# 512-column float32r matmuls of a transformer's projections as two of 256 columns on the same weights

## The reference

```python
h = rms_norm(x, norm1_gain[l]) * (1.0 + sc1) + sh1
z = h @ w_in[l]                       # 1024 x 4408
...
merged = sigmoid(g_mla_merge) * y_mla + sigmoid(g_nsa_merge) * y_nsa
x = x + gt1 * (merged @ w_out[l])
h2 = rms_norm(x, norm2_gain[l]) * (1.0 + sc2) + sh2
x = x + gt2 * ((silu(h2 @ ffn_w_gate[l]) * (h2 @ ffn_w_up[l])) @ ffn_w_down[l])
```

## Time and profile before

| | |
|---|---|
| median of 3 runs | 2311.57 us (2309.75 to 2312.49) |
| the profiled execution, first to last instruction | 2308.2 us |
| TensorE busy | 2253.8 us, 98% |
| weight loads busy | 1799.2 us, 78% |
| VectorE, ScalarE, GpSimd busy | 947.8, 612.0, 1393.4 us |
| matmuls recorded | 10597 |

### The profile page before, as it was taken

One profiled execution on the slowest core, in us unless ns is written; L12 is line 12 of the kernel. 1 busy time (PEld: TensorE's weight loads), 2 busy tenths in 40 slices (PEclk: granted clock), 3 DMA queues, 4 the chain that ended last, 5 costly groups with the idle time before them and its releaser, 6 DMA issues.

```text
span 2308.2 us, 28721 instructions
## 1 busy us (share of the span) xinstructions
PE 2253.8 (98%) x10597; PEld 1799.2 (78%) x10597; DVE 947.8 (41%) x1742; ACT 612.0 (27%) x1335; POOL 1393.4 (60%) x522
## 2 busy tenths in 40 slices
PE   7999999999999999999999999999999999999997
PEld 5787887787888888787787788888787787888885
DVE  6744777544110132325636433302235627433202
ACT  3263652112111100104643222201015623222200
POOL 4755404776777777774018777777773038777773
PEclk9999999999999999999999999999999999999999
DMA  8322103422222232222002222222221012222221
GB/s 327 128 74 92 56 20 114 176 80 75 103 91 91 96 146 109 92 91 73 1 19 73 105 95 91 92 91 91 91 91 55 1 37 74 94 101 96 91 91 55
DMA packets 32725, 206.08 MB, mean 89 GB/s; under 512 B 4080, under 2 KB 4336, under 8 KB 11632
## 3 DMA queue, kind: packets, MB, share of 16 engines
q1 hardware_dynamic: 32192, 200.27, 24.1%
q10 hardware_dynamic: 432, 4.46, 0.5%
HBM read 202.61 MB, written 2.10 MB: 89 GB/s over the span
## 4 chain that ended last, share of the span: by engine, by line
PE 92%; DVE 3%; POOL 1%; issue 1%; ACT 1%; DMA 0%; DVEq 0%; ACTq 0%; SPq 0%; POOLq 0%
PE PS L756 25%; PE PS L758 25%; PE PS L757 25%; PE PS L1052 5%; PE PS L1078 4%; PE PS L1067 2%; PE PS L1025 1%; PE PS L828 1%; PE PS L770 1%; POOL w_hi L426 1%; POOL w_lo L430 1%; PE PS L1108 1%; DVE ring L1997 1%; PE PS L1337 0%; DMA xT<-xT_dram 0%
## 5 line engine op out<-in xcount | busy, mean ns | idle before, releaser
L426 POOL TENSOR_TENSOR w_hi<-raw,zero_c 128x2048 fp32r<-128x2048 f32 (+1 forms) x238 | 593.7, 2508 | 834.0 <-PE PS L758 832.7
L430 POOL TENSOR_TENSOR w_lo<-raw,w_hi 128x2048 fp32r<-128x2048 f32 (+1 forms) x238 | 757.4, 3197 | 12.4
L756 PE MATMUL PS<-f_hi,w_hi 128*128 128x512 f32 x992 | 393.5, 397 | 2.1 <-POOL w_lo L430 1.4
L758 PE MATMUL PS<-f_hi,w_lo 128*128 128x512 f32 x992 | 393.3, 396 | 0.0
L757 PE MATMUL PS<-f_lo,w_hi 128*128 128x512 f32 x992 | 393.2, 396 | 0.0
L756 PEld LDWEIGHTS PS<-f_hi,w_hi 128*128 128x128 f32 x992 | 186.8, 188 | 48.8 <-POOL w_lo L430 2.3
L758 PEld LDWEIGHTS PS<-f_hi,w_lo 128*128 128x128 f32 x992 | 186.8, 188 | 45.6
L757 PEld LDWEIGHTS PS<-f_lo,w_hi 128*128 128x128 f32 x992 | 186.8, 188 | 45.3
L756 PE MATMUL PS<-a_hi,w_hi 128*128 (+1 forms) x528 | 209.7, 397 | 0.0
L757 PE MATMUL PS<-a_lo,w_hi 128*128 (+1 forms) x528 | 209.3, 396 | 0.0
L758 PE MATMUL PS<-a_hi,w_lo 128*128 (+1 forms) x528 | 209.3, 396 | 0.0
(11 more groups left out here) (424 smaller groups left out, 3692.4 us busy)
## 6 DMA issues: line engine op xcount, KB each, us to landing
raw<-slabs_dram SPq DMA_DIRECT2D x161, 1024.0 KB, 4.8
aux<-ada_dram SPq DMA_DIRECT2D x18, 512.0 KB, 5.1
ada_first<-ada_dram SPq DMA_DIRECT2D x11, 512.0 KB, 14.1
cmpw<-cmpw_dram ACTq DMA_DIRECT2D x2, 2048.0 KB, 11.6
ada_late<-ada_dram SPq DMA_DIRECT2D x8, 512.0 KB, 3.3
ada_last<-ada_dram SPq DMA_DIRECT2D x8, 512.0 KB, 6.1
xT<-xT_dram SPq DMA_DIRECT2D x1, 2048.0 KB, 9.1
out_dram<-t SPq DMA_DIRECT2D x4, 512.0 KB, 2.7
```

The source lines that it names most:

```text
L426: high = nc.gpsimd.tensor_tensor(w_hi[:, slot, c], raw[:, slot, c], zero[:, 0:c.stop - c.start], ALU.add)
L430: low = nc.gpsimd.tensor_tensor(w_lo[:, slot, c], raw[:, slot, c], w_hi[:, slot, c].bitcast(f32), ALU.subtract)
L756: nc.tensor.matmul(out, a_hi_, b_hi_, start=start, stop=False)
L758: return nc.tensor.matmul(out, a_lo_, b_hi_, start=False, stop=stop)
```

## The change

`three` makes each of its three products as two matmuls where the output has 512 columns: first columns 0 to 255, then 256 to 511, with the same stationary tile and the same PSUM bank. The narrower ones (384 and 312 columns) stay whole. The flag that starts an accumulation is set on the very first of the six alone, the one that ends it on the last alone, and it is the last that the semaphore increments hang on. No wait, buffer, transfer or instruction of another engine changes.

```diff
             def three(out, a_hi_, a_lo_, b_hi_, b_lo_, start, stop):
-                nc.tensor.matmul(out, a_hi_, b_hi_, start=start, stop=False)
-                nc.tensor.matmul(out, a_hi_, b_lo_, start=False, stop=False)
-                return nc.tensor.matmul(out, a_lo_, b_hi_, start=False, stop=stop)
+                n = out.shape[-1]
+                for a, b in ((a_hi_, b_hi_), (a_hi_, b_lo_), (a_lo_, b_hi_)):
+                    for c in (slice(0, n // 2), slice(n // 2, n)) if n == 512 else (slice(0, n),):
+                        first, final = b is b_hi_ and a is a_hi_ and c.start == 0, a is a_lo_ and c.stop == n
+                        last = nc.tensor.matmul(out[:, c], a, b[:, c], start=start and first, stop=stop and final)
+                return last
```

## The result

The kernel with the halves is **slower**: 2331.7 us median (2326.5 to 2335.2, four runs) against 2312.0 us (2309.8 to 2312.7, four runs) for the kernel before in the same job, ratio 1.0089 with a 95% interval of 1.0074 to 1.0104. Forecast was 2243 us. The profiled execution spans 2330.6 us, 22.4 more than the one of before.

A forecast was written before the change was run, and what follows sets the result against it. TensorE's instruction stream bounds the kernel; 7488 split matmuls at -0.0093 us each give -70 us, -68 after small losses, so 2240 us profiled and 2243 us median, 3.0% less; range 2230 to 2350.

The forecast's parts named there:

- T256: Start-to-start time of a 256-column float32r matmul: forecast 0.1125 us, range 0.109 to 0.120, break-even at 0.1172.
- Rival 1: Matmuls of `three`: about 13 ns fixed price each plus 0.417 ns a column; +43 us, 2355 us; chance 0.11.
- Rival 2: Split matmuls pay float32's price, two halves costing 3 ns more than one whole; +22 us, 2334 us; chance 0.08.
- A constant rate: Third rival, split matmuls: cost proportional to columns, 0.1172 us for 256; within 1 us of 2312; chance 0.05.
- rival 4: Weight load and matmul lose time handing over: +103 us, 2414, chance 0.07; milder -32 us, 2280, 0.11 shared with full refetching.
- rival 5: The second half's weight load is dropped, its weights being in place; -122 us, 2190 us; chance 0.06.
- (a): First two slabs run at VectorE's pace, so their 96 matmuls give nothing; 0.9 us lost.
- (b): GpSimd's weight splitting stays covered in each slab; its idle time falls from 3.0 to about 2.5 us.
- (c): Slab transfers stay covered: 4.8 us from issue to landing, wanted once in 10.8 us.
- (d): TensorE's waits at stage ends can grow by a few tenths each, 1 us together.
- (e): The attentions are float32 matmuls of other lines and don't change.
- (f): Up-projection loops of 384 matmuls a pass: resident at no cost, otherwise refetching costs 12 to 24 us, 2255 to 2267.

The follow-up runs named there:

- the bench: Rows of like matmuls added behind the last barrier of the kernel before, other engines idle; 512 columns take 234.4 ns there, and whole-kernel times say nothing.
- shifted kernel: Kernel before or after with its arena moved 32, 64, 96 or 224 bytes; at 96 bytes 2265.1 us without halves, 2351.3 us with them.

## Why the prediction was wrong

- **The bound and the count: right.** TensorE's stream is the kernel's time before and after, 7488 more matmuls and loads came, and 76% of the chain lies on them.
- **T256, the step that failed.** The prediction drew a line through 512 and 384 columns and read 0.1125 us off it. Measured are 0.1167 to 0.1200 in after. The mean over all pairs is 0.1184, and the error 2 x 0.0059 x 7488 = 88 us, from -70 to +19, where +19.9 were measured. The line through 312 and 384 was the better one: its slope, 0.417 ns a column with 13.3 ns on top, holds from 288 to 448 columns at the kernel's place. It is 512 that is off it, by 7.7 ns, and that surplus goes when the tiles lie at d = 0. I had argued against this line that it puts 512 columns at 0.2267 us while thousands take 0.2343; 0.2267 is just what they take at d = 0.
- **The 312-column row.** I set it aside as one that counts like 320 columns. It doesn't: 312 take 144.0 ns and 320 take 146.7 on the same tiles. That the place of the data matters was right, but what counts is the distance of the two tiles and not a row's multiple of 64 bytes. The inference, which set one row of three aside, carried the whole forecast.
- **The bounds: right, and they held the result.** Below: the weight load at 0.109 to 0.112 us (the bench has 0.1116 for 128 to 240 columns). Above: 0.120, the dearest form of after. So the range of 2230 to 2350 has 2331.7 in it, but two thirds of the chance lay on the wrong side.
- **Rival 1 had the arithmetic**, a fixed part for each matmul and something else on 512, with a size to correct: 256 columns are off the line too, downwards, so that at d = -96 a half is 118.3 and not 120.0. It gave 2355; at +96 bytes, where 256 columns take the full 120.0, the kernel takes 2351.3. It had 0.11, and the rows then at hand gave it at least as much as the line that was taken. That the time came out near the middle between it and no change is the place of the tiles, of which no rival knew. **Rival 2** has the right time (2334) by a wrong cause: float32 pays 2 x 215.8 - 429.2 = +2.4 ns a pair in the bench, and its 512 columns take 429 ns in every shifted kernel (256 were tried at one place only), while the float32r pair goes from -6.8 ns (2 x 113.3 - 233.4) to +13.3 (2 x 120.0 - 226.7). By the Trainium skill (TensorE: Matmul & The Clock Gate, Back-to-back issue gap) the gap of an isolated warm matmul is N / 2.4 + 2.5 ns, 215.8 for 512 columns. The trace disagrees for float32r: the lowest value of a row here is 226.7.
- **Rivals 3 to 5.** A constant rate (0.1172) is nearly what the last stages and `g` show, but 384 columns are not on it (0.1757 by the rule, 0.1733 measured), and at another place neither is 256: luck, not a rule. The lockstep of loads and matmuls (rival 4) didn't show: 64 loads at 0.1116 us run beside matmuls of 128 to 240 columns. The second load (rival 5) is not dropped: there are as many loads as matmuls.
- **The small terms.** (a), (b), (c) rest on less time for a slab and were not put to the test; GpSimd's idle time stayed at 2.9 to 3.0 us, as the slab took no less. (d) TensorE's waits at the ends of stages did not grow: w_lo is at 1.9 us in total for 2.5, h_lo at 4.0 for 4.3. The 2.6 us outside the float32r stretches lie in the attentions, of which (e) says that they don't change; most are transposes. With one trace of each kernel it stays open whether the change made them.
- **(f) Instructions: answered.** A loop of 384 matmuls and as many loads stays resident: no packet of q8 in 650 to 780 us, nor in 1340 to 1470 and 2035 to 2165, inside the other two loops; over the program there are 103, for 64 before. The Trainium skill (Runtime: NRT & Kernel Launch, Instruction fetch mechanics) gives TensorE room for 2048 instructions. The trace agrees. What a refetch would have cost (the 1 to 2 us a packet of the prediction) no run shows.

**What stays open**: why the distance counts modulo 256 bytes, why the order of the places is another one for 512 than for 256 columns (at d = 0 the first are cheapest and the second dearest, at d = 64 both are cheap), and what picks one of two paces. That the weight load and the moving tile's reads get into each other's way in SBUF would fit (fewer stationary columns made 512 cheaper), but none of the runs separates it from other causes. The table above is measured; a rule behind it is not.

**A better version.** `shift96_before`, the kernel before with its arena 96 bytes further and no halves, takes 2265.1 us (2263.3 to 2267.7): 2.1% less than before, from two edited numbers. 4560 of its matmuls (`f` and `a` moving) went from 234.3 to 226.7 ns and 1152 (`f` stationary) from 233.4 to 227.1: 34.7 + 7.3 = 42 us. `o`, `m`, `u` and `OmT` give 6 more, and in the trace the work between the projections is 3 us longer: 45 of the 46 that were measured.

## What to carry to other kernels

A line through two widths is not a price: before splitting or merging matmuls, measure the new width itself, with the stationary and the moving tile at the places that they have in the kernel. If TensorE's stream is the bound, the place of the tiles is a parameter to sweep (here 8 ns of 234 for each matmul, 2% of the kernel, for one constant), and a difference of a few ns a matmul between two versions may come from there and not from the edit. The best place depends on the width, so a sweep holds for one width only. And when one of three rows contradicts the line that the forecast rests on, the forecast is worth no more than the reason for setting that row aside.

## What was unexpected of the hardware

- A float32r matmul of 288 to 448 columns (128 rows, 128 stationary columns) takes N / 2.4 + 13.3 ns from start to start at d = -96, at a granted clock of 1.00, and up to about 3 ns more at the other places tried. One of 512 takes 226.7 to 234.6 and one of 256 takes 113.3 to 120.0, ordered by the distance of the two tiles modulo 256 bytes; at d = 0, where 512 is cheapest, 256 is among the dearest.
- Weight loads of 188 ns in the record run side by side with the matmuls; bench rows of 240, 192 and 128 columns all cost 111.2 to 111.7 ns a matmul, so that splitting further gives nothing below 240.
- One form at one place can run at two paces, 117.3 and 118.7 ns or 113.3 and 117.8, kept over a stretch of matmuls and in the kernel over hundreds of microseconds; what picks the pace is not known.
